# Latent attention on one core: scores from high and low fp32r halves, key norm factors applied to the scores

## What is computed

```python
def mla_queries(h, wq_a, q_a_norm, wq_b, q_norm):
    cq = rmsnorm(h @ wq_a, q_a_norm)
    q = (cq @ wq_b).reshape(B, S, MLA_HEADS, QK_DIM)
    return rmsnorm(q, q_norm)

def mla_keys_values(h, wkv_a, kv_a_norm, wkv_b, k_norm):
    kv_a = h @ wkv_a
    ckv, k_pe = kv_a[..., :KV_LORA], kv_a[..., KV_LORA:]
    kv = (rmsnorm(ckv, kv_a_norm) @ wkv_b).reshape(B, S, MLA_HEADS, QK_NOPE + V_DIM)
    k_nope, v = kv[..., :QK_NOPE], kv[..., QK_NOPE:]
    k_pe = jnp.broadcast_to(k_pe[:, :, None, :], (B, S, MLA_HEADS, QK_ROPE))
    k = rmsnorm(jnp.concatenate([k_nope, k_pe], axis=-1), k_norm)
    return k, v
...
    k_lat = rope_part(k_lat, cos, sin)
    q_lat = rope_part(mla_queries(h_lat, wq_a, q_a_norm, wq_b, q_norm), cos, sin)
    o_lat = block_attention(q_lat, k_all, v_all, scale).reshape(B, S, MLA_HEADS * V_DIM) @ wo
...
        s = jnp.einsum('bqhd,bkhd->bhqk', qi, k) * scale
        p = jax.nn.softmax(s, axis=-1)
        return jnp.einsum('bhqk,bkhd->bqhd', p, v)
```

## Time and profile before

| | |
|---|---|
| median of 3 runs | 1016.6 us (1011.88 to 1020.12) |
| the profiled execution's own time | 1011.75 us |
| its span in the profile | 1009.9 us |
| PE busy, share of the span | 957.0 us, 95% |
| DVE | 721.5 us, 71% |
| ACT | 522.3 us, 52% |
| POOL | 291.4 us, 29% |
| mean granted TensorE clock | 0.977 of full speed |
| chain that ended last | PE 79%, DVE 12%, ACT 4%, issue 3% |

### The profile page before, as it was taken

One profiled execution on the slowest core, in us unless ns is written; L12 is line 12 of the kernel. 1 busy time (PEld: TensorE's weight loads), 2 busy tenths in 40 slices (PEclk: granted clock), 3 DMA queues, 4 the chain that ended last, 5 costly groups with the idle time before them and its releaser, 6 DMA issues.

```text
span 1009.9 us, 19412 instructions
## 1 busy us (share of the span) xinstructions
PE 957.0 (95%) x6858; PEld 867.5 (86%) x6858; DVE 721.5 (71%) x1124; ACT 522.3 (52%) x889; POOL 291.4 (29%) x252
## 2 busy tenths in 40 slices
PE   5988999999999999989889999999999989899995
PEld 5977534699999999968879999999999867899994
DVE  3997778777988777687876787555555785375865
ACT  3465344465765444554544666654445673464553
POOL 1942000137996111120051288631110000120022
PEclk9799999999999999999989999999999999899998
DMA  8856233168887787579525676555555423055421
GB/s 342 285 195 250 84 125 127 50 227 301 305 281 274 271 281 284 196 267 328 185 87 170 227 272 207 180 176 187 189 185 177 134 94 111 21 170 190 144 83 42
DMA packets 55339, 194.54 MB, mean 193 GB/s; under 512 B 5999, under 2 KB 8463, under 8 KB 54896
## 3 DMA queue, kind: packets, MB, share of 16 engines
q1 hardware_dynamic: 54880, 192.36, 54.9%
q0 software_dynamic: 400, 1.39, 0.5%
HBM read 192.65 MB, written 1.07 MB: 192 GB/s over the span
## 4 chain that ended last, share of the span: by engine, by line
PE 79%; DVE 12%; ACT 4%; issue 3%; POOL 1%; DMA 1%; SPq 0%; DVEq 0%; ACTq 0%
PE bank L508 23%; PE bank L509 22%; PE bank L510 22%; DVE w_lo L1476 2%; ACT w_hi L1082 2%; PE bank L745 1%; DVE products L1578 1%; PE bank L606 1%; PE bank L728 1%; PE bank L727 1%; DVE ada_raw L1578 1%; DMA x<-x_in 1%; PE bank L701 1%; PE bank L777 1%; PE bank L901 1%
## 5 line engine op out<-in xcount | busy, mean ns | idle before, releaser
L1476 DVE TENSOR_TENSOR w_lo<-raw,w_hi 128x1024 fp32r<-128x1024 f32 (+1 forms) x261 | 338.4, 1299 | 119.0 <-ACT w_hi L1082 116.7
L1082 ACT ACTIVATE w_hi<-raw 128x1024 fp32r<-128x1024 f32 (+1 forms) x261 | 271.8, 1043 | 160.7 <-PE bank L510 148.7
L508 PE MATMUL bank<-act_hi,w_hi 128*128 128x258 f32 (+1 forms) x872 | 251.3, 288 | 0.0
L509 PE MATMUL bank<-act_lo,w_hi 128*128 128x258 f32 (+1 forms) x872 | 248.1, 285 | 0.0
L510 PE MATMUL bank<-act_hi,w_lo 128*128 128x258 f32 (+1 forms) x872 | 247.6, 284 | 0.0
L508 PEld LDWEIGHTS bank<-act_hi,w_hi 128*128 128x128 f32 x872 | 166.1, 190 | 3.2 <-issue 2.3
L509 PEld LDWEIGHTS bank<-act_lo,w_hi 128*128 128x128 f32 x872 | 166.1, 190 | 1.0 <-issue 1.0
L510 PEld LDWEIGHTS bank<-act_hi,w_lo 128*128 128x128 f32 x872 | 166.1, 191 | 0.0
L509 PE MATMUL bank<-hid_lo,w_hi 128*128 128x256 f32 x512 | 143.9, 281 | 0.0
L510 PE MATMUL bank<-hid_hi,w_lo 128*128 128x256 f32 x512 | 143.4, 280 | 0.0
L508 PE MATMUL bank<-hid_hi,w_hi 128*128 128x256 f32 x512 | 142.3, 278 | 0.0
(11 more groups left out here) (314 smaller groups left out, 1789.3 us busy)
## 6 DMA issues: line engine op xcount, KB each, us to landing
raw<-weights SPq DMA_DIRECT2D x247, 512.0 KB, 3.8
ada_raw<-ada SPq DMA_DIRECT2D x88, 512.0 KB, 4.9
raw<-weights SPq DMA_DIRECT2D x14, 384.0 KB, 4.3
ada_more<-ada SPq DMA_DIRECT2D x8, 512.0 KB, 5.0
bias<-bias_by_distance SPq DMA_DIRECT2D x1, 2048.0 KB, 9.3
x<-x_in SPq DMA_DIRECT2D x1, 1024.0 KB, 7.5
ctx<-ctx_in SPq DMA_DIRECT2D x1, 1024.0 KB, 9.5
out<-result SPq DMA_DIRECT2D x1, 1024.0 KB, 3.8
```

The costliest lines, as they stand in the source:

```text
L508: pe.matmul(dst, w[0], a[0], start=start, stop=False)
L509: pe.matmul(dst, w[0], a[1], start=False, stop=False)
L1082: act.activation(w_hi[:, slot, 0:width_of(c)], raw[:, slot, 0:width_of(c)], ACT.Copy).then_inc(weight_hi, 1)
L1476: dve.tensor_tensor(w_lo[:, slot, 0:w], raw[:, slot, 0:w], w_hi[:, slot, 0:w].bitcast(fp32), ALU.subtract).then_inc(weight_lo, 1)
```

## The change

- The nope queries stay in two fp32r halves (`qn_hi`, `qn_lo`, which lie in the free `act_hi` and `act_lo`), so do the rotated queries, the keys and the rotated key part. The scores are six fp32r matmuls (two `split_product`s) instead of two fp32 products.
- The keys are no longer multiplied by their norm factor; `gqk` (the product of the two gains) goes in when the bank is read. `key_spread` works on fp32r halves of the reciprocal, `key_factor(h)` on ScalarE copies the spread factor to SBUF, and a fused pass on VectorE (L1783 of the changed kernel) multiplies the scores by it, writes the result to `logit_mla` and gives its maximum. The exponential reads `logit_mla`, and the next scores into a bank wait for this pass, not for the exponential.
- q_b: the rope groups come first, four banks. ScalarE makes square and high half, VectorE (`query_low`) the low half from the bank.
- kv_b_k: ScalarE squares and makes the high half, VectorE (`key_low`) the low half, the sums stand between the products of later heads and the rotations ahead of all of them.
- `modulate` 3 to 9 come later, and 7 and more lie in or just ahead of the loop.

The diff, cut to its core (declarations and waits on them are left out):

```diff
-                n, col, sel = (1, i, ones[:, 0:1]) if i < H else (2, H + 2 * (i - H), const[:, P + 16:P + 18])
+                n, col, sel = (1, i - 4, ones[:, 0:1]) if i >= 4 else (2, H + 2 * i, const[:, P + 16:P + 18])
...
+            def query_group(g):
...
+            for i in range(6):
+                query_group(2 * i)
+                query_group(2 * i + 1)
...
+            def key_sums(h):
                 pe.wait_ge(k_squared, h + 1)
                 pe.matmul(bank[4][0:H, :], one_column(h), sq_k(h), start=False,
                           stop=h == H - 1).then_inc(k_sums, 1)
+            pe.wait_ge(split_lo, split0["ckv"] + 4)
+            for h in range(H):
...
+                pe.wait_ge(evacuated, n - 1)
+                for k in range(2):
+                    last = split_product(bank[n % 2][:], weight(c, (h % 4 * 2 + k) * P, P),
+                                         (ckv_hi[:, k, :], ckv_lo[:, k, :]), k == 0, k == 1)
+                last.then_inc(matmul_steps, 1)
+                if h >= 2:
+                    key_sums(h - 2)
+            key_sums(H - 2)
+            key_sums(H - 1)
...
-                pe.matmul(bank[spread_bank(h)][:], ident[0:H, h:h + 1].to_broadcast([H, P]), rstd[0:H, :],
-                          start=True, stop=True).then_inc(k_spread, 1)
+                    pe.wait_ge(k_factor, h - 1)
+                head = heads[:, h:h + 1].to_broadcast([H, P])
+                pe.matmul(bank[spread_bank(h)][:], head, k_rstd_hi[:], start=True, stop=False)
+                pe.matmul(bank[spread_bank(h)][:], head, k_rstd_lo[:], start=False, stop=True).then_inc(k_spread, 1)
...
-                    pe.wait_ge(latent.probs, u - 1)
-                pe.matmul(bank[4 + u % 2][:], qn[:, h, tok], kn[:, h, :], start=True, stop=False)
-                pe.matmul(bank[4 + u % 2][:], qr[r, h // 2, tok], kr[r, h // 2, :],
-                          start=False, stop=True).then_inc(latent.scores, 1)
+                    pe.wait_ge(latent.logits, u - 1)
+                q, k_ = (qn_hi[:, h, tok], qn_lo[:, h, tok]), (kn_hi[:, h, :], kn_lo[:, h, :])
+                split_product(bank[4 + u % 2][:], q, k_, True, False)
+                q, k_ = (qr_hi[r, h // 2, tok], qr_lo[r, h // 2, tok]), (kpe_hi[r, :], kpe_lo[r, :])
+                split_product(bank[4 + u % 2][:], q, k_, False, True).then_inc(latent.scores, 1)
...
+            pe.wait_ge(kpe_ready, 1)
             pe.wait_ge(q_ready, 1)
+            pe.wait_ge(k_std, 1)
             latent_scores(0)
             latent_scores(1)
-            key_spread(2)
             for u in range(2 * H):
-                if u % 2 == 1 and u // 2 + 3 < H:
-                    key_spread(u // 2 + 3)
                 if u + 2 < 2 * H:
                     latent_scores(u + 2)
                 latent_turn(u)
+                if u % 2 == 1 and u // 2 + 2 < H:
+                    key_spread(u // 2 + 2)
                 if u % 2 == 0 and u > 0:
                     latent_values(u // 2 - 1)
...
-                    if g < H:
-                        evacuate("q_b", g, qn[:, g, :], square=sq[:, (g + 3) % 8, :], bank_=g % 3)
+                    if g < 4:
+                        evacuate("q_b", g, qr[:, g, :], scale=V("q_g_rope"), square=sq[:, (g + 3) % 8, :], bank_=g)
                     else:
-                        evacuate("q_b", g, qr[:, g - H, :], scale=V("q_g_rope"), square=sq[:, (g + 3) % 8, :],
-                                 bank_=g % 3)
+                        act.wait_ge(matmul_steps, after_group[group0["q_b"] + g])
+                        act.activation(sq[:, (g + 3) % 8, :], bank[g % 4][:, 0:S], ACT.Square)
+                        act.activation(qn_hi[:, g - 4, :], bank[g % 4][:, 0:S], ACT.Copy).then_inc(q_high, 1)
...
-            for i in range(2):
-                for g in range(4 * i, 4 * i + 4):
-                    evacuate("kv_b_k", g, kn[:, g, :], width=SC)
-                convert(chunk0["kv_b_k"] + i + 4)
+            act.wait_ge(gqk_ready, 1)
+            for h in range(H):
+                n = group0["kv_b_k"] + h
+                act.wait_ge(matmul_steps, after_group[n])
+                if h >= 4:
+                    act.wait_ge(k_sums, h - 3)
+                act.activation(sq_k(h), bank[n % 2][:], ACT.Square).then_inc(k_squared, 1)
+                act.activation(kn_hi[:, h, :], bank[n % 2][:], ACT.Copy, scale=gqk[:]).then_inc(k_high, 1)
+                if h % 4 == 3:
+                    convert(chunk0["kv_b_k"] + h // 4 + 4)
+                if h == 4:
+                    act.wait_ge(kpe_turned, 1)
+                    act.activation(kpe_hi[:], kpe, ACT.Copy).then_inc(kpe_high, 1)
...
+            def key_factor(h):
+                act.wait_ge(k_spread, h + 1)
+                if h >= 4:
+                    act.wait_ge(latent.logits, 2 * h - 6)
+                act.activation(sq_k(h), bank[spread_bank(h)][:], ACT.Copy).then_inc(k_factor, 1)
...
-                act.activation(p_mla[:, u % 2, :], bank[4 + u % 2][:], ACT.Exp, bias=small[:, 48 + u:49 + u],
+                act.activation(p_mla[:, u % 2, :], logit_mla[u % 2], ACT.Exp, bias=small[:, 48 + u:49 + u],
...
+            def query_low(h):
+                g = 4 + h
+                dve.wait_ge(q_high, h + 1)
+                dve.wait_ge(evacuated, group0["q_b"] + g)
+                dve.tensor_tensor(qn_lo[:, h, :], bank[g % 4][:, 0:S], qn_hi[:, h, :].bitcast(fp32),
+                                  ALU.subtract).then_inc(evacuated, 1)
...
-            then(dve.tensor_tensor(gqk[:], V("q_g_nope"), V("k_g_nope"), ALU.mult))
-            modulate(3)
+            dve.tensor_tensor(gqk[:], V("q_g_nope"), V("k_g_nope"), ALU.mult).then_inc(gqk_ready, 1)
+            convert(13)
+            query_low(0)
+            query_low(1)
             dve.wait_ge(lora_std, 1)
             dve.reciprocal(rstd[:], std[:]).then_inc(lora_rstd, 1)
-            convert(13)
+            query_low(2)
             dve.wait_ge(lora_rstd, 1)
             for k in range(4):
...
+                if k == 1:
+                    query_low(3)
             convert(14)
+            query_low(4)
+            convert(15)
+            query_low(5)
+            modulate(3)
+            convert(16)
+            query_low(6)
+            query_low(7)
             modulate(4)
-            convert(15)
-            modulate(5)
-            convert(16)
-            modulate(6)
             convert(17)
...
-            for h in range(H):
-                dve.wait_ge(evacuated, group0["kv_b_k"] + h + 1)
-                if h >= 4:
-                    dve.wait_ge(k_sums, h - 3)
-                dve.tensor_tensor(sq_k(h), kn[:, h, :], kn[:, h, :], ALU.mult).then_inc(k_squared, 1)
-                if h == 3:
-                    convert(18)
-                    modulate(7)
-                    modulate(8)
-                    modulate(9)
-            convert(19)
-            dve.wait_ge(rotated, 1)
-            dve.wait_ge(rope_in, 16)
+            def key_low(h):
+                n = group0["kv_b_k"] + h
+                dve.wait_ge(k_high, h + 1)
+                dve.scalar_tensor_tensor(kn_lo[:, h, :], bank[n % 2][:], gqk[:], kn_hi[:, h, :].bitcast(fp32),
+                                         ALU.mult, ALU.subtract).then_inc(evacuated, 1)
             def rotate(p_):
...
-                then(dve.tensor_tensor(v, v, p_mla[:, 0, 0:S], ALU.add))
-            rotate(4)
-            dve.wait_ge(k_std, 1)
-            dve.reciprocal(rstd[0:H, :], std[0:H, :]).then_inc(k_rstd, 1)
-            for p_ in range(4):
-                rotate(p_)
+                return dve.tensor_tensor(v, v, p_mla[:, 0, 0:S], ALU.add)
+            dve.wait_ge(rope_in, 16)
+            for h in range(H):
+                key_low(h)
+                if h == 0:
+                    dve.wait_ge(rotated, 1)
+                    rotate(4).then_inc(kpe_turned, 1)
+                    dve.wait_ge(kpe_turned, 1)
+                if h in (1, 2, 4):
+                    then(rotate((0, 0, 1, 0, 2)[h]))
+                if h == 3:
+                    convert(18)
+                if h == 5:
+                    rotate(3).then_inc(qr_turned, 1)
+                if h == 6:
+                    dve.wait_ge(kpe_high, 1)
+                    dve.tensor_tensor(kpe_lo[:], kpe, kpe_hi[:].bitcast(fp32), ALU.subtract).then_inc(kpe_ready, 1)
+            modulate(5)
+            convert(19)
...
-            dve.tensor_scalar(q_scale[:, 1], q_scale[:, 0], -1.0, None, ALU.mult).then_inc(q_ready, 1)
-            dve.wait_ge(q_ready, 1)
-            def final_key(h):
-                r = slice((h % 2) * ROPE, (h % 2 + 1) * ROPE)
-                dve.wait_ge(k_spread, h + 1)
-                dve.scalar_tensor_tensor(kn[:, h, :], kn[:, h, :], gqk[:], bank[spread_bank(h)][:], ALU.mult, ALU.mult)
-                dve.tensor_tensor(kr[r, h // 2, :], kpe[r, :], bank[spread_bank(h)][r, :], ALU.mult).then_inc(k_ready, 1)
```

(28 more changed lines are left out.)

75 lines of the change are left out of this document (51 added, 24 removed).

## The result

| | before | after |
|---|---|---|
| median of 14 runs each, us | 1019.5 | 1011.5 |
| lowest and highest, us | 1011.7, 1025.2 | 1007.4, 1015.5 |
| profiled execution, us (span) | 1011.75 (1009.9) | 1015.5 (1013.7) |
| mean granted clock of that execution | 0.977 | 0.968 |

The ratio is 0.992, with a 95% interval from 0.990 to 0.995: faster by 0.8%. The forecast of 1008.0 is 3.5 us low; its range, 1001 to 1015.5, holds the result. A second set of six runs of the changed kernel gave 1009.2 beside 1020.6 (0.989, 0.986 to 0.992).

The account below looks back on a forecast made before the run. TensorE was taken as the bound, busy 957.0 of 1009.9 us, VectorE close behind in the loop. Terms -0.2 - 1.3 - 7.0 gave -8.5 at `mla_out`, from the median 1016.6 to 1008; range 1001 to 1015.5.

Parts of the forecast that it names:

- query and key stages: Query projection to the end of the key products: +0.1 for the query stage, +1.8 us for change-overs and a bank wait.
- value stage: Value products up to the first scores: cheaper factor spreads -1.1 us, a TensorE wait for late key factors +1.5.
- first scores to first turn: Start of the head loop: VectorE's chain puts the first turn 6.5 us after the first scores, against 9.2.
- first two units: Start of the loop: paced by VectorE, 5.4 us for 6.7, so -1.3.
- five heads: Head loop up to the turn at 184.15: TensorE at 6.4 us per head, 32.0 for 38.97, so -7.0.
- tail: From 184.15 to 195.17, a chain of last scores, turn, copy and values: 0.
- sum at `mla_out`: First product of `mla_out`: -0.2 - 1.3 - 7.0 = -8.5 us, a start at about 186.7.
- The stages ahead: Query, key and value stages before the loop: first scores +2.3, say +2.5 us late, bounds +0.5 and +4.5.
- two change-overs into fp32r 0.22: TensorE's work per head in the loop: 0.22 us for changes from fp32 into fp32r, within 6.39 for 7.97.
- fourth rival: Fp32r products of 64 rows or a stationary of 8 cost 0.34 each: gain -4, 1012.6 us; chance 0.07.
- first rival: VectorE takes over the loop if the fused pass costs 1.31: 6.9 us per head, gain -5, 1011.6; chance 0.12.
- third rival: TensorE gaps drop its clock to 1.2 GHz in the loop: slower, 1033 us with half the loop's work; chance 0.05.

Follow-up runs that it names:

- the five whose factors come first: Changed kernel with the key factors' reciprocal earlier on VectorE: alone, median 1009.03 us; in four versions also with query heads 6 and 7 earlier, 1001.9 to 1006.3.
- the other profile before: The kernel before, no edit, profiled once more: 1020.42 us.
- the filled opening: Kernel before, with VectorE's third key eviction and two weight conversions at the loop's head moved behind the first normalisation: median 1013.68 us beside 1020.71.
- The run with 128 rows: Changed kernel, with rope products reading all 128 rows instead of their head's 64, so the scores are other numbers: median 1008.31 us beside 1009.21.
- the changed kernel's repetition: The changed kernel again, no edit: median 1009.21 us, the profiled run 1007.06.
- the one with 2.35: Changed kernel, with one more VectorE modulation step ahead of the loop's first normalisation: median 1015.86 us beside 1009.21.
- both 128-row versions: Rope products over 128 rows, in the changed kernel alone (median 1008.31 us) and with factor reciprocal and query heads 6 and 7 first (1001.9).

## Why the prediction came out as it did

The total was near and the sum under it was not. Counted from the common product, so without the 0.87 us of a later start:

| term | forecast | measured |
|---|---|---|
| query and key stages | +1.9 | 121.52 - 0.87 - 115.86 = +4.8 |
| value stage | +0.6 | 15.55 for 13.41 = +2.1 |
| first scores to first turn | 6.5 for 9.2 | 6.48 for 9.19 |
| first two units | -1.3 | 5.65 for 6.72 = -1.1 |
| five heads | -7.0 | 183.86 - 149.20 = 34.66 for 38.97 = -4.3 |
| tail | 0 | 10.69 for 11.02 = -0.3 |
| sum at `mla_out` | -8.5 | -1.5 |

**The stages ahead** failed by 4.4 us. The waits themselves were right: 2.73 in the query stage (some idle there was expected), 0.87 for `kn_lo` (0.75), 1.33 for `k_rstd_lo` (1.5). What failed is the clock behind them. The wait for the factors was given only its own length, and a new stretch of 3.4 us stood behind it (+1.7): it is there in all six profiles with that wait and in none of the five whose factors come first. In the query stage the clock fell again, as expected, but for 6.8 us where the profile before had 3.4 (+1.7). That difference is not the work of the change: the other profile before has 6.8 us there too, and the one with the filled opening, the same program up to the loop, 6.9. The profile that was read was the rare one here as well. Of the remaining 1.0 or so about half is in the key stage. Five more changes into fp32 and back are there, as forecast:

```profile
106.06 1.02 PE L712 MATMUL bank<-sq,const 128*8 128x512 f32 x2
107.01 0.50 PE L519 MATMUL bank<-om_hi,w_hi 128*128 128x512 f32 x1
...
109.57 0.50 PE L519 MATMUL bank<-om_hi,w_hi 128*128 128x512 f32 x1
```

A head takes 2.56 us, for 1.40 of products and 0.87 of sums: 0.29 for the change there and back, where 0.2 was booked. The rest is not assigned.

**The five heads** failed at "two change-overs into fp32r 0.22" in the sum of 6.39; a head took 6.93, and 6.20 without the changes to 64 rows. The fourth rival had the right shapes with the wrong mechanism: it is not each 64-row or 8-row product that costs more, but each change from one row count to another. The run with 128 rows settles it.

**VectorE and the opening** held: the fused pass 0.77 with its read against 0.85, 5.6 us of VectorE per head against 5.8, the first turn 6.5 behind the first scores (the terms listed for it add up to 6.2; the other 0.3 has no source). The first rival had no part in it.

**The median** was taken as 1016.6 - 8.5, and this step was right by luck. The forecast took every saved us from a profile in which the clock held through the loop. In most executions it did not, behind the loop's first wait, and what the change gives there is the half-speed stretch of 6.5 us, and 1.5 to 2.1 us of distance. Against the second profile before the changed kernel's repetition has a distance of 118.00 for 127.44, 9.4 us less: 14.5 in the loop, less 5.0 ahead of it. The forecast's 8.5 is near that, from other terms. In five profiled executions with the wait of 1.16 the stretch does not come, in the one with 2.35 it does. The third rival looked for the clock in the loop of the changed kernel, with "1.00 in the loop with its wait of 1.85" as the row against it; it never asked whether that row was typical of the kernel before. Its mechanism exists, and works for the change.

**What stays open.** The two profiles before have the same wait of 1.85 and differ in the clock behind it, and both 128-row versions held their clock behind one of 1.94; in the query stage a stretch came with no wait over 0.29. The length of the wait alone does not decide, and no run shows what else does. That most executions before have the stretch in the loop rests on their times, one profile and the filled opening's 7.0 us. Nor was one of the runs before at 1024 us profiled. The profiled run of the changed kernel lost further time outside the attention (819.15 us from `mla_out` to the end, 812.56 in its repetition), for example here, where that repetition has a clock of 1.00 at the same place in the program:

```profile
438.00:448.00 10.00, 7.86 (x27) 5.68 (x26) 8.22 (x11) 6.17 (x10) 3.44 (x4) 0.83 0.72 245
818.00:832.00 14.00, 12.18 (x46) 8.36 (x45) 9.91 (x34) 9.89 (x33) 0.73 (x1) 0.76 0.24 77
```

Why it comes there in one run and not in the next was not tested.
